# First head of a two-block kernel: x by its root on VectorE with shift and scale on ScalarE, weight splits on VectorE, p's high part ahead of tanh, the residual's squares on ScalarE

## The reference, cut to what matters

```python
mod = c @ ada_w[l] + ada_b[l]
sh1, sc1, gt1, sh2, sc2, gt2 = [m[:, None, :] for m in jnp.split(mod, 6, axis=-1)]
h = rmsnorm(x, norm1_g[l]) * (1.0 + sc1) + sh1
p = h @ w_in[l]
xr, yr, q, k, v, ga, gb = jnp.split(p, cuts, axis=-1)
...
y_a = rg_lru(xr, ...) * jax.nn.gelu(yr)
y_b = stick_breaking_attention(q, k, v)
mix = jax.nn.sigmoid(ga) * y_a + jax.nn.sigmoid(gb) * y_b
x = x + gt1 * (mix @ w_out[l])
h2 = rmsnorm(x, norm2_g[l]) * (1.0 + sc2) + sh2
```

## Time and profile before

| | |
|---|---|
| median of 3 runs | 2004.26 us (2004.02 to 2007.66) |
| the profiled execution's own time | 2006.96 us |
| its span, first to last instruction | 2004.9 us |
| mean granted TensorE clock | 0.985 of full |
| TensorE (matmuls) | 1935.7 us busy, 97% |
| VectorE | 968.4 us, 48% |
| ScalarE | 907.0 us, 45% |
| GpSimd | 800.4 us, 40% |
| first head's matmuls | 29.1 to 76.65 us |
| heads' loop and last head | to 505.1 us |
| next matmul with weights | 521.8 us |

### The profile page before, as it was taken

The page is one execution under the profiler, slowest core; times in us unless marked ns, Lnnn a source line. Parts: engine busy times, 40 slices in busy tenths (PEclk is TensorE's granted clock), DMA queues, the critical chain, the costliest instruction groups (busy, mean ns, idle before and its releaser), DMA issues.

```text
span 2004.9 us, 25312 instructions
## 1 busy us (share of the span) xinstructions
PE 1935.7 (97%) x8720; PEld 1573.5 (78%) x8720; DVE 968.4 (48%) x1140; ACT 907.0 (45%) x1204; POOL 800.4 (40%) x365
## 2 busy tenths in 40 slices
PE   4999999999899999999999999999999999999998
PEld 4777777777688888888888888787777788888887
DVE  6766666666544343222434422346777544434322
ACT  4477777775355554223223222366676322223222
POOL 2233333333244444444444445533332434444443
PEclk9999999999899999999999999999999999999998
DMA  7333333333122222232232233222221222223231
GB/s 287 105 115 126 123 119 118 121 116 126 53 94 102 97 94 94 98 101 85 96 101 96 94 105 105 84 84 74 84 73 64 74 84 94 94 98 101 95 105 73
DMA packets 54471, 203.15 MB, mean 101 GB/s; under 512 B 6048, under 2 KB 6176, under 8 KB 53280
## 3 DMA queue, kind: packets, MB, share of 16 engines
q1 hardware_dynamic: 54432, 202.62, 29.5%
HBM read 200.50 MB, written 2.10 MB: 101 GB/s over the span
## 4 chain that ended last, share of the span: by engine, by line
PE 85%; DVE 7%; ACT 5%; issue 2%; DMA 1%; ACTq 0%; POOL 0%; POOLq 0%; DVEq 0%; SPq 0%
PE bank L612 24%; PE bank L613 24%; PE bank L617 24%; PE bank L963 1%; PE bank L965 1%; PE bank L964 1%; DVE PARTS L1751 1%; DVE TG L1565 1%; PE bank L761 1%; PE bank L996 1%; PE bank L725 1%; DVE MIX L1565 1%; PE bank L753 1%; ACT ARENA L1238 1%; ACT WH L1113 1%
## 5 line engine op out<-in xcount | busy, mean ns | idle before, releaser
L506 POOL TENSOR_TENSOR WL<-ring,WH 128x1024 fp32r<-128x1024 f32 (+2 forms) x326 | 777.7, 2386 | 1150.1 <-ACT WH L1113 1150.1
L1113 ACT ACTIVATE WH<-ring 128x1024 fp32r<-128x1024 f32 (+2 forms) x326 | 338.9, 1042 | 868.8 <-PE bank L617 775.8
L612 PE MATMUL bank<-HH,WL 128*128 128x512 f32 x1744 | 690.0, 396 | 7.1 <-POOL WL L506 3.8
L613 PE MATMUL bank<-HH,WH 128*128 128x512 f32 x1744 | 684.6, 393 | 0.0
L617 PE MATMUL bank<-HL,WH 128*128 128x512 f32 x1744 | 431.7, 389 | 0.5 <-DVE HL L1565 0.5
L612 PEld LDWEIGHTS bank<-HH,WL 128*128 128x128 f32 x1744 | 331.2, 190 | 77.2 <-POOL WL L506 5.2
L613 PEld LDWEIGHTS bank<-HH,WH 128*128 128x128 f32 x1744 | 330.9, 190 | 68.0
L617 PEld LDWEIGHTS bank<-HL,WH 128*128 128x128 f32 x1744 | 327.4, 188 | 69.5 <-DVE HL L1565 1.7
L613 PE MATMUL bank<-FH,WH 128*128 128x512 f32 x544 | 211.6, 389 | 0.0
L612 PE MATMUL bank<-FH,WL 128*128 128x512 f32 x544 | 211.6, 389 | 0.0
L617 PE MATMUL bank<-FL,WH 128*128 128x512 f32 x544 | 135.0, 389 | 0.0
(11 more groups left out here) (324 smaller groups left out, 2099.8 us busy)
## 6 DMA issues: line engine op xcount, KB each, us to landing
ring<-in_stream SPq DMA_DIRECT2D x355, 512.0 KB, 3.3
ARENA<-in_ada SPq DMA_DIRECT2D x8, 1024.0 KB, 13.5
ring<-in_stream SPq DMA_DIRECT2D x8, 448.0 KB, 10.6
XT<-in_xt SPq DMA_DIRECT2D x1, 2048.0 KB, 7.9
result<-XT SPq DMA_DIRECT2D x3, 512.0 KB, 2.7
result<-XT SPq DMA_DIRECT2D x2, 256.0 KB, 2.1
vec<-in_vec SPq DMA_DIRECT2D x1, 220.0 KB, 2.5
```

The source lines that it names most:

```text
L506: nc.gpsimd.tensor_tensor(WL[:, slot, 0:cols], ring[:, u % RING, 0:cols], WH[:, slot, 0:cols].bitcast(F32), ALU.subtract).then_inc(w_low, 1)
L612: mm(out_ap, part(WL, base, loc, k), xh(k), start=(start and k == 0), stop=False)
L613: mm(out_ap, part(WH, base, loc, k), xh(k), start=False, stop=False)
L1113: A(WH[:, split_at(base, loc)[1], 0:cols], ring[:, u % RING, 0:cols], ACT.Copy).then_inc(w_high, 1)
```

## The change

- **x** is loaded by two DMAs of four tiles each with a semaphore of its own; ScalarE squares the first half without the second.
- **First head, VectorE and ScalarE.** VectorE multiplies x by the root alone (`first_normed`), which needs no modulation and stands ahead of MOD. Gain and shift are scale and bias of ScalarE's Identity, which is run twice per tile: for HH, and for the full h, written over MIX. HL is their difference (`first_h_low`).
- **First head, weight splits** of the 8 units move from GpSimd to VectorE (`first_low`); GpSimd waits until `w_low` is 8 before the second head's.
- **First head, columns.** Row 7 of each group no longer goes through VectorE: TensorE multiplies the group's rows 7 by c[7] into the same columns and adds TG's sums. The columns stand behind the 14 matmuls with HH instead of among them. SP's fourth group waits for the first pair's columns.
- **Heads.** PH is ScalarE's next operation behind the two sigmoids; tanh stands with exp (`decays`).
- **Residual.** ScalarE squares x into MIX; VectorE adds 0 to 6 into SS, TensorE takes SS and tile 7 (16 records instead of 24). The squares 0 to 5, a weight copy, the squares 6 and 7 and the root stand ahead of the second weight copy for the FFN. The clearing of SS goes, and `CLEAR` counts one less.

```diff
-            sp.dma_start(XT[:, :], xt_in).then_inc(x_in_s, 16)
+            for half, x_s in ((slice(0, KD * S // 2), x_in_s), (slice(KD * S // 2, KD * S), x_second_s)):
+                sp.dma_start(XT[:, half], xt_in[:, half]).then_inc(x_s, 16)
 
...
-                    sp.wait_ge(first_sum, KD - 1)
+                    sp.wait_ge(ada_col, 4)
                     first_group(GROUP_BUFFERS)
...
-            for k in range(KD):
-                split(U_FIRST, k, k, cols=FIRST_COLS)
+            pool.wait_ge(w_low, KD)
...
-                for i, T in enumerate((SS[:, :], CG[:, 0, :], CG[:, 1, :])):
-                    if i:
-                        pe.wait_ge(sq_done, SQ_BEFORE[n] + 4 * i)
+                parts = ((SS[:, :], 0), (tile_of(MIX, KD - 1), 8)) if n == 1 else ((SS[:, :], 0), (CG[:, 0, :], 4), (CG[:, 1, :], 8))
+                for i, (T, squares) in enumerate(parts):
+                    if squares:
+                        pe.wait_ge(sq_done, SQ_BEFORE[n] + squares)
                     for t in range(NT):
                         last = mm(bank[SUM_BANK[n]][:, t:t + 1], T[:, t * P:(t + 1) * P], ones[:, 0:1],
-                                  start=(i == 0 and t == 0), stop=(i == 2), skip_group_check=True)
+                                  start=(i == 0 and t == 0), stop=(i == len(parts) - 1), skip_group_check=True)
...
             def first_columns(p):
 
-                pe.wait_ge(first_sum, (KD - 1) * (p + 1))
+                pe.wait_ge(ada_arrived[2 * p + 1], 16)
+                pe.wait_ge(vec_in_s, 16)
                 if p:
                     pe.wait_ge(mod_done, p)
+
+                def to(j):
+                    col = 2 * p + j // 2 + KD * (j % 2)
+                    return bank[6][:, col:col + 1]
                 for j in range(4):
-                    col = 2 * p + j // 2 + KD * (j % 2)
-                    mm(bank[6][:, col:col + 1], TG[:, p % 2, j * P:(j + 1) * P], ones[:, 0:1],
-                       start=True, stop=True).then_inc(ada_col, 1)
+                    mm(to(j), group_rows(p, KD - 1)[:, j * P:(j + 1) * P], v("c", KD - 1),
+                       start=(j == 0), stop=False, skip_group_check=True)
+                pe.wait_ge(first_sum, FIRST_SUMS * (p + 1))
+                for j in range(4):
+                    mm(to(j), TG[:, p % 2, j * P:(j + 1) * P], ones[:, 0:1],
+                       start=False, stop=True, skip_group_check=True).then_inc(ada_col, 1)
...
                 if k < KD - 1:
                     for j, b in enumerate(FIRST_BANK):
-                        if k % 2 and j == 4:
-                            first_columns((k + 1) // 2)
                         mm(bank[b][:, :], first_part(WL, j), tile_of(HH, k), start=(k == 0), stop=False)
                         mm(bank[b][:, :], first_part(WH, j), tile_of(HH, k), start=False, stop=False)
+                    if k % 2:
+                        first_columns((k + 1) // 2)
                     pe.wait_ge(h_low, k + 1)
                     for j, b in enumerate(FIRST_BANK):
                         last = mm(bank[b][:, :], first_part(WH, j), tile_of(HL, k), start=False, stop=False)
...
-            act.wait_ge(x_in_s, 16)
             for k in range(KD):
+                if k % 4 == 0:
+                    act.wait_ge(x_second_s if k else x_in_s, 16)
                 A(tile_of(MIX, k), tile_of(XT, k), ACT.Square).then_inc(sq0_done, 1)
...
-                A(TG[:, p % 2, :], group_rows(p, 0), ACT.Copy, scale=v("c", 0)).then_inc(first_row, 1)
...
             def h_of(k):
                 act.wait_ge(h_mul, k + 1)
-                A(tile_of(HH, k), tile_of(MIX, k), ACT.Identity, bias=MOD[:, k:k + 1]).then_inc(h_high, 1)
+                act.wait_ge(gain_done, k // 2 + 1)
+                A(tile_of(HH, k), tile_of(MIX, k), ACT.Identity, bias=MOD[:, k:k + 1], scale=G1[:, k:k + 1]).then_inc(h_high, 1)
+                A(tile_of(MIX, k), tile_of(MIX, k), ACT.Identity, bias=MOD[:, k:k + 1], scale=G1[:, k:k + 1]).then_inc(h0_done, 1)
 
...
             for p in range(GROUPS):
                 if p:
                     first_high(2 * p)
                 h_of(2 * p)
+                if p:
+                    first_high(2 * p + 1)
                 h_of(2 * p + 1)
                 if p < GROUPS - 1:
                     first_scaled(p + 1)
-                if p:
-                    first_high(2 * p + 1)
...
             def gate_parts(h):
+
                 A(M["RG"], bank[5][:, :], ACT.Sigmoid, bias=vd("rg_ba", h)).then_inc(q["rg_sig"], 1)
                 A(M["IG"], bank[7][:, :], ACT.Sigmoid, bias=vd("rg_bx", h)).then_inc(q["ig_sig"], 1)
+                act.wait_ge(q["p_done"], 3 * h + 3)
+                A(M["PH"], M["PP"], ACT.Copy).then_inc(q["ph_done"], 1)
+
+            def decays(h):
                 act.wait_ge(q["rg_sig"], h + 1)
                 A(M["TH"], M["RG"], ACT.Tanh, scale=nc8[:, bass.ds(h, 1)]).then_inc(q["th_dec"], 1)
-
-            def p_high(h):
-                act.wait_ge(q["p_done"], 3 * h + 3)
-                A(M["PH"], M["PP"], ACT.Copy).then_inc(q["ph_done"], 1)
                 A(M["AD"], M["RG"], ACT.Exp, scale=c8[:, bass.ds(h, 1)]).then_inc(q["a_dec"], 1)
...
-                p_high(h)
...
+
+            def square(m):
+                act.wait_ge(res_done, 8 + m + 1)
+                A(tile_of(MIX, m), tile_of(XT, m), ACT.Square).then_inc(sq_done, 1)
+
+            for m in range(6):
+                square(m)
             out1_finished(O6)
             weight_high(U_UP1, 0)
+            square(6)
+            square(7)
+            norm(1, eps1)
             out1_finished(O7)
             weight_high(U_UP1, 1)
-            norm(1, eps1)
...
             def first_rows(p, first, end):
                 for k in range(first, end):
                     dve.wait_ge(ada_arrived[2 * p + k // 4], 16)
-                    if k == 1:
-                        dve.wait_ge(first_row, p + 1)
-                    else:
-                        dve.wait_ge(first_sum, (KD - 1) * p + k - 1)
+                    dve.wait_ge(first_sum, FIRST_SUMS * p + k)
                     STT(TG[:, p % 2, :], group_rows(p, k), v("c", k), TG[:, p % 2, :], ALU.mult, ALU.add).then_inc(first_sum, 1)
+
+            def first_low(k):
+                dve.wait_ge(w_high, k + 1)
+                TT(WL[:, k % 2, 0:FIRST_COLS], ring[:, k % RING, 0:FIRST_COLS], WH[:, k % 2, 0:FIRST_COLS].bitcast(F32),
+                   ALU.subtract).then_inc(w_low, 1)
...
+            def first_normed(k):
+                if k == 0:
+                    dve.wait_ge(rs_copied, 1)
+                TT(tile_of(MIX, k), tile_of(XT, k), SQ[:, :], ALU.mult).then_inc(h_mul, 1)
+
+            def first_h_low(k):
+                dve.wait_ge(h_high, k + 1)
+                dve.wait_ge(h0_done, k + 1)
+                TT(tile_of(HL, k), tile_of(MIX, k), tile_of(HH, k).bitcast(F32), ALU.subtract).then_inc(h_low, 1)
+
             first_rows(0, 1, 4)
             inverse(0)
-            first_rows(0, 4, KD)
+            first_rows(0, 4, KD - 1)
+            first_low(0)
             for p in range(GROUPS):
+                first_normed(2 * p)
+                first_normed(2 * p + 1)
                 dve.wait_ge(ada_col, 4 * (p + 1))
...
                 STT(G1[:, at], MOD[:, KD + 2 * p:KD + 2 * p + 2], one[:, :], v("norm1_g", 2 * p, 2), ALU.add, ALU.mult).then_inc(gain_done, 1)
-                dve.wait_ge(gain_done, p + 1)
-                dve.wait_ge(rs0_copied, 1)
-                for k in (2 * p, 2 * p + 1):
-                    STT(tile_of(MIX, k), tile_of(XT, k), G1[:, k:k + 1], SQ[:, :], ALU.mult, ALU.mult).then_inc(h_mul, 1)
-                low(2 * p, 0, tile_of(MIX, 2 * p), lambda k: MOD[:, k:k + 1])
-                low(2 * p + 1, 0, tile_of(MIX, 2 * p + 1), lambda k: MOD[:, k:k + 1])
+                if p == 0:
+                    first_low(1)
+                first_h_low(2 * p)
+                if p:
+                    first_low(2 * p + 1)
+                first_h_low(2 * p + 1)
                 if p < GROUPS - 1:
-                    first_rows(p + 1, 1, KD)
-
-            dve.wait_ge(first_sum, GROUPS * (KD - 1))
+                    first_rows(p + 1, 1, 5)
+                    first_low(2 * p + 2)
+                    first_rows(p + 1, 5, KD - 1)
+
+            dve.wait_ge(first_sum, GROUPS * FIRST_SUMS)
+            dve.wait_ge(ada_col, 4 * GROUPS)
...
                 STT(x, bank[OUT1_BANK[m]][:, :], MOD[:, ADA_FIRST + m:ADA_FIRST + m + 1], x, ALU.mult, ALU.add).then_inc(res_done, 1)
-                dve.wait_ge(res_done, 8 + m + 1)
-                if m % 4 == 3:
-                    TT(CG[:, m // 4, :], x, x, ALU.mult).then_inc(sq_done, 1)
-                    continue
-                TT(SQ[:, :], x, x, ALU.mult).then_inc(sq_done, 1)
-                dve.wait_ge(sq_done, SQ_BEFORE[1] + m + 1)
-                TT(SS[:, :], SS[:, :], SQ[:, :], ALU.add).then_inc(ss_done, 1)
```

(7 more changed lines are left out.)

20 lines of the change are left out of this document (11 added, 9 removed).

## The result

The changed kernel takes **1981.36 us** (median of 4 runs, 1979.98 to 1984.04), the kernel before beside it 2004.14: ratio 0.9885, 95% interval 0.9868 to 0.9902, so 22.8 us less. The forecast was 18.4 us, and its range ended 1.6 us too high. The profiled execution took 1981.78 us, its span is 1980.1, the mean granted clock 0.989. All ratios compare fast executions alone; one of e8's four was slow (2432.23 us, clock 0.75) and is left out.

A forecast was written before the change was run, and what follows sets the result against it. TensorE is busy for 97% of the span, so only its waits can be won. First head 5.0, p's high part 3.6 and residual 9.8 make 18.4 us: 2004.26 to 1985.9 us, range 1983.0 to 1992.0.

The forecast's parts named there:

- p's high part: Heads 0 to 6: run ahead of tanh, it ends TensorE's wait for p's low part; 3.6 us, bounds 0 and 4.3.
- Drain and refill: Heads: a drain of 0.1 us behind each wait might go too, which gives the bound of 4.3 us.
- First head: Start and first head: first matmul 5.2 us earlier, end at 71.5 instead of 76.65; 5.0 us gained.
- first matmul: First head: TensorE's first matmul at about 23.9, where it was at 29.1; 5.2 us earlier.
- MOD of the first pair: First head: ready at 22.7 instead of 26.99, and for the fourth pair at 60.8 instead of 64.26.
- splits: First head: VectorE's 128x896 weight split takes 1.09 us in proportion, between 0.69 and 1.49.
- the periods: First head, from G to G: 12.7 us each, three times 38.1 us, not shorter than before.
- What GpSimd's lock costs now, VectorE spends on the splits: First head: moving the weight splits to VectorE leaves the period no shorter, at 12.7 us.
- Residual: Last output matmul to first product: some 4.7 us instead of 15, squares on ScalarE; 9.8 us gained.
- The rivals: First head gives little 0.14; heads' wait replaced 0.12; residual's sum late 0.08; ScalarE squares slow 0.02; clock slows TensorE 0.04.
- the trace shows it at 3.3 us alone: First head: a TensorE wait of 3.28 us halved the clock, one of 1.09 us in the last head did not.
- Signs named ahead: Wrong if: TG rows above 2 us, clock below 0.9 between 29 and 71, new head wait of 0.3 us, late sum.

The follow-up runs named there:

- e8: The changed kernel with the first head's weight splits back on GpSimd, the rest as changed: ratio 0.9926 (0.9904 to 0.9947).
- e1: The kernel before with p's high part ahead of tanh in all heads, and no other part of the change: ratio 0.9969, 6.2 us.
- e11: The changed kernel itself once more, beside the same runs of the kernel before: ratio 0.9882 (0.9865 to 0.9898).
- e3: The kernel before with the new first head alone: ratio 0.9977 (0.9967 to 0.9986), 4.6 us.
- e6: The changed kernel with 26 and 5 added TensorE products of ident and ones that compute nothing, at the start: ratio 0.9887 (0.9872 to 0.9902).

## Why the prediction was wrong

The direction, the three places and their order of size were right; the sum was 4.4 us short. By its steps:

- **p's high part: the step that failed.** "The wait goes: **3.6 us** over seven heads", bounded by 4.3. The runs show 6.2 us (stretch of the table, and e1), and this is the largest part of the 4.4. The mechanism was right, its price was that of the idle row, 0.50 us a head. What TensorE lost is the difference between the way that set its time (14.46 us, over ScalarE) and its own (13.48), and the period changed by 0.95. Drain and refill (0.22) were put at 0.1 and as a bound only. The 0.23 us at the projection, a late weight part that cost nothing before since TensorE would have waited later anyway, was not seen at all.
- **First head: 5.0 forecast, 6.3 as a mean.** (The prediction's own times, 76.65 and 71.5, give 5.15.) The steps came close: first matmul 23.39 for 23.9, MOD of the first pair 21.92 for 22.7, of the fourth 60.03 for 60.8, splits 1.08 for 1.09. Two errors cancel in the periods: the first took 14.1 us, the others 12.0, where 12.7 stood for each. The first k piece ran at half clock from 23.39 to 29.1, and ScalarE's copy of tile 2's weights waited for it (31.20). The first period moves with that clock: 13.6 us in e11, 12.9 in e3. In the profiled pair the gain is 3.98 us, less than forecast, since the clock fell once more at 59.86. The trace of before was a lucky one here: head 0's mark at 107.11, where four other traces with the old first head have 108.29 to 109.83. A forecast from one profiled execution inherits that.
- **"What GpSimd's lock costs now, VectorE spends on the splits"** holds for the rows and low parts alone (2.3 us against 2.2). It left out that one split of two stands in a wait of VectorE and is free, and that GpSimd's way leaves TensorE longer pauses: e8 loses some 8 us.
- **Residual: 9.8 forecast, 10.3 measured.** Square 0.63 us, 8 columns 1.05 and spread 1.16 at full clock, where slower ones were allowed for. The Trainium skill's page "ScalarE: Activation LUTs" (Rules for kernel authors) gives multiplications to VectorE, with up to about three times its speed in bf16 for operations with one input. It states no factor for float32 with two inputs, and here the rows say 0.63 us on ScalarE against 0.69 on VectorE. Sums were slow beside GpSimd's splits twice (2.23 and 2.54 us), where the prediction had one; both ended ahead of TensorE's last matmul.
- **The rivals.** None came. In the changed kernel no other wait took the place of the one in the heads. The clock did not fall in every pause of the first head (0.42 and 0.46 us before the columns, with one fall behind the second), but behind the first k piece it fell once or twice in each of the nine traces with the new first head. The prediction's "the trace shows it at 3.3 us alone" misread the trace of before: behind the 24 single-column matmuls of the second block, with no pause, it has matmuls at half clock too (0.63 us each from 1637.65 on).
- **Signs named ahead:** rows of TG stayed at 0.83 us, no wait for PARTS, no new wait in the heads. The granted clock between 59 and 65 us was 0.72, below 0.9, the sign for "wrong". In the seven matmuls at 59.86 alone it cost 1.46 us, more than the 1.2 us by which the end at 72.67 missed 71.5.

## To carry to other kernels

Price a wait by two ways from the same release: that of the engine waited for, and that of the waiting engine by itself, including everything behind that has been late without cost. The idle row showed 0.50 of 0.95 us here. Where GpSimd and VectorE both read two inputs on the critical way, count which engine starts first, and take three traces of the kernel before, if they are to be had, before one stage of one trace is used as the base.

## Unexpected

- GpSimd's weight split and VectorE's rows meet in a window of tenths of a us: in the trace of before the seventh row started 0.18 us ahead of the split (split 2.82 us), in e1 0.04 us behind it (split 2.39, row delayed). Why the change of phase comes with a shorter period wasn't isolated.
- A fall of the clock came behind pauses as short as 0.4 us (59.86, changed kernel; 47.2 in e11), not behind another of the same length (0.42 us up to 46.96, changed kernel), and behind none at all (1616.7). Ahead of each of these falls TensorE ran single-column matmuls; whether they bring it about was not isolated. Over fourteen traces the unchanged stretch behind the residual has 1479.7 to 1484.8 us.
- A 128x128 float32 product of two float32 operands ran as two matmuls, 0.112 us from start to start at full clock and 0.213 at half (e6; its expectation had 0.107 and 0.26).
